# Query heads paired c with c+8 on the row halves of the array, and the decode value product on four column tiles

## The chip, the cores and the metric

The kernel runs on one core of one Trainium2 chip. A core has a matrix engine (TensorE, in the profile PE for its matmuls and PEld for its weight loads), a vector engine (DVE), an activation engine (ACT), GpSimd (POOL) and a queue engine that only issues transfers (SP). The metric is the time of one execution in microseconds (us), lower is better.

## What is computed

A two-layer decoder step for a prompt of 2048 tokens and for 64 sample tokens (8 sequences of 8). Layer 0 is a gated depthwise convolution of width 31. Then keys and values are made once, with 4 key heads of 64 numbers. Layer 1 has 16 query heads; query head h reads key head h // 4, over a window of 128 tokens, with one extra weight (a sink) per head in the softmax. The lines that matter here:

```python
# heads: N_HEADS = 16, N_KV_HEADS = 4, HEAD_DIM = 64, GROUP = 4, WINDOW = Q_BLOCK = 128
q = rms_norm(q.reshape(b, t, N_HEADS, HEAD_DIM), q_norm_g)
k = rms_norm(k.reshape(b, t, N_KV_HEADS, HEAD_DIM), k_norm_g)
s = jnp.einsum('bqkgd,bskd->bkgqs', qg, k_ctx) * (HEAD_DIM ** -0.5)
s = s - alibi_slopes()[..., None, None] * dist
s = jnp.where(allowed, s, -jnp.inf)
m = jnp.maximum(jnp.max(s, axis=-1, keepdims=True), sink)
p = jnp.exp(s - m)
p = p / (jnp.sum(p, axis=-1, keepdims=True) + jnp.exp(sink - m))
o = jnp.einsum('bkgqs,bskd->bqkgd', p, v_ctx)
return x + jnp.einsum('bte,ed->btd', o * jax.nn.silu(z), w_out)
```

## The kernel before

The program has three phases, one after another, and each engine runs an instruction list written out by hand; semaphores are the only thing that holds an engine back. Phase A is layer 0 up to the convolution. Phase B is the rest of layer 0, the keys and values and the queries; it writes queries (`q_d`), keys and values (`kv_d`) to memory, 17 tiles of 128 tokens (the last holds the 64 sample tokens). Phase C is the attention with the gate `z` and the output projection, 16 tiles of 128 prompt tokens. All large products are made of a high and a low part of both factors (`project`, 24 matmuls of 512 columns a call).

A tile `t` of phase C handles the 16 heads as four groups of four (`kv` 0 to 3). On TensorE the body of a tile runs: `qk` group 0 (scores), `z` first half (24 matmuls), `qk` group 1, `turn_p` group 0 (four transposes of the softmax), `z` second half, `pv` group 0 (value product, ahead of it two transposes of the gate), `qk` 2, `turn_p` 1, `out` of the tile before, first half, `pv` 1, `qk` 3, `turn_p` 2, `out` second half, `pv` 2, `turn_p` 3, then `turn_q` and `turn_k` for the next tile (8 and 4 transposes), `pv` 3. A score matmul needs its 64 key dimensions on the same half of the array's rows as its 64 query dimensions, and neighbouring query heads (2c and 2c+1) sit on the two halves. Both belong to one key head, so every key head is needed on both halves: `load_k` writes each key head twice (tile `c_kd`, two transfers a tile), `turn_k` transposes four 128x128 blocks of it into PSUM (`c_acc`), and ACT copies them into `c_kt` (`keys`). `c_kt` is a ring; on tiles with an even number the copy is made twice (slots 0 and 2). ACT does `queries(t+1)` and `keys(t+1)` one after the other, and `qk` of the next tile and its `z` wait for `kt_ready`.

Tiles 6 to 13 also carry one sample sequence each (b = 0 to 7): `decode_keys`, `decode_qk` (four products on tiles of 64 rows and 32 columns of the array), `decode_turn`, `decode_pv`, `decode_back`, with DVE and ACT steps in between. `decode_pv` multiplies the 128 rows of softmax (16 heads x 8 tokens) with all four value heads, 256 columns, although each row needs 64 of them; `decode_norm` then takes the four diagonal blocks out, one DVE instruction for each.

At the change from phase B to C the weights of the gate (`w_in_b`, 16 pieces of 128x512) are loaded, cut into high (ACT, `split_weights_hi`, line 101) and low parts (DVE, line 109), through four staging slots (`c`/`b_gate`) that SP fills when DVE has freed them. SP issues everything in order: between these pieces it also issues keys, `c_ht` and the store of the last queries.

Of the kernel before, what the change touches and what calls it, by code (L numbers as in the profile page):

```python
# [14 lines left out]
P = 128  # L15
# [64 lines left out]

def split_weights_dma(sp, weights, g, n0, k0=0, k1=KT):

    for k in range(k0, k1):
        piece = KT * n0 + k
        after(sp, g.w_lo, piece - g.stages + 1)
        sp.dma_start(g.stage[:, piece % g.stages], weights[k * P:(k + 1) * P, :]).then_inc(g.w_in[piece % g.stages], 16)

# [5 lines left out]

def split_weights_hi(act, m, gain, g, n0, free=None, k0=0, k1=KT):
# [9 lines left out]
def split_weights_lo(dve, m, gain, g, n0, k0=0, k1=KT):  # L104

    for k in range(k0, k1):
        piece = KT * n0 + k
        dve.wait_ge(g.w_hi, piece + 1)
        dve.scalar_tensor_tensor(g.wslot[m][:, 1, k], g.stage[:, piece % g.stages],  # L109
                                 gain_of(gain, k), f32(g.wslot[m][:, 0, k]),  # L110
                                 ALU.mult, ALU.subtract).then_inc(g.w_lo, 1)

# [658 lines left out]
def phase_b(nc, io, g, ctx, prev):  # L771
# [499 lines left out]
    def vector(dve, gates):  # L1271
# [90 lines left out]
        def queries(t):  # L1362
            n = rows_of(t)
            dve.wait_ge(qrs_ready, t + 1)
            rs = hrs[0:n, 0:HEADS].rearrange("p (h a) -> p h a", a=1).broadcast_to([n, HEADS, HD])
            given = qo if n == DEC else ps_q
            dve.tensor_tensor(heads(qo[0:n], HEADS), heads(given[0:n], HEADS), rs, ALU.mult).then_inc(q_ready, 1)

# [237 lines left out]
def phase_c(nc, io, g, ctx, prev):  # L1606
# [124 lines left out]
    def sync(sp):  # L1731
# [71 lines left out]
        def body(t, r):  # L1803
# [46 lines left out]
    def scalar(act):  # L1850
# [81 lines left out]
        def gates(first, stop):  # L1932
            w.stage = prev.gate_stage
            for k in range(first, stop):
                split_weights_hi(act, Z0 + k // KT, prev.gain, w, k // KT, k0=k % KT, k1=k % KT + 1)

# [68 lines left out]
    def vector(dve):  # L2005
# [13 lines left out]
        def scores(G, t, kv, b, r):  # L2019
# [3 lines left out]
            for j in range(GROUP):  # L2023
                if starts(t):
                    to, far, given = s[:, b, place(j)], dist[:, P:2 * P], ps_s[:, place(j), 0:P]
                else:
                    to = s[:, b:3:2 - b, place(j)]
                    far, given = (ap.rearrange("p (a n) -> p a n", a=2) for ap in (dist[:, :], ps_s[:, place(j)]))
                ins = dve.scalar_tensor_tensor(to, far, -slope[kv * GROUP + j], given, ALU.mult, ALU.add)  # L2029
            ins.then_inc(s_read, 1)  # L2030
# [86 lines left out]
        def decode_norm(b):  # L2117
            dve.wait_ge(d_pe, PE0 + PES * b + 4)
            dve.wait_ge(d_dve, DVE0 + DVES * b + 6)
            for kv in range(KVH):  # L2120
                rows = slice(kv * GROUP * DS, (kv + 1) * GROUP * DS)
                part = ps_tf[rows, CT * P + kv * HD:CT * P + (kv + 1) * HD].rearrange("p (a d) -> p a d", a=1).broadcast_to([GROUP * DS, 2, HD])
                ins = dve.tensor_scalar(sd[rows, 0:P].rearrange("p (a d) -> p a d", a=2), part, rdend[rows, 0:1], None, ALU.mult)
            ins.then_inc(d_dve, 1)

        def decode_gated(b):
# [3 lines left out]
            for e in range(2):  # L2130
                rows = slice(e * HD, (e + 1) * HD)
                part = szd[rows, :, b * DS:(b + 1) * DS]
                ins = dve.tensor_tensor(part, ps_t[rows, CT + 2].rearrange("p (k e i) -> p k e i", k=KT, e=2)[:, :, e], part, ALU.mult)
            ins.then_inc(d_dve, 1)
# [5 lines left out]
        def gates(first, stop):  # L2140
            w.stage = prev.gate_stage
            for k in range(first, stop):
                split_weights_lo(dve, Z0 + k // KT, prev.gain, w, k // KT, k0=k % KT, k1=k % KT + 1)

# [3 lines left out]
        ordered = lambda ap: ap.rearrange("p (g b a) -> p g b a", b=2, a=2)  # L2148
        given = sink0[:, :].rearrange("p (g a b) -> p g b a", b=2, a=2)
        dve.tensor_scalar(ordered(sink[:, :]), given, 1.0, None, ALU.mult).then_inc(nsink_made, 1)  # L2150
# [101 lines left out]
    def tensor(pe):  # L2252
# [7 lines left out]
        def turn_k(t, p):  # L2260
            pe.wait_ge(k_in[p], 32 * (t // 2 + 1) if isinstance(t, int) else t * 16 + (32 if p == 0 else 16))
# [57 lines left out]
        def qk(t, kv, r):  # L2319
# [4 lines left out]
            for a in range(2):  # L2324
                for half in range(2):
                    for e in range(2):
                        rows, h = slice(e * HD, (e + 1) * HD), kv * GROUP + 2 * a + e
                        keys = kt[rows, kv, window(t, r)].rearrange("p a n -> p (a n)")
                        to = ps_s[half * HD:(half + 1) * HD, place(2 * a + e), span_of(t, half)]
                        ins = pe.matmul(to, qt[rows, h // 2, half * HD:(half + 1) * HD], keys[:, span_of(t, half)], start=True, stop=True)  # L2330
            ins.then_inc(qk_done, 1)
# [9 lines left out]
        def pv(t, kv, r, loads):  # L2341
# [237 lines left out]
```

## Time and profile before

| | |
|---|---|
| median of three runs | 1718.73 us (1717.98, 1718.73, 1722.67) |
| the profiled execution's own time | 1717.28 us |
| its span, first to last instruction | 1715.5 us (1.8 us lie around it) |
| PE busy in the span | 1653.8 us (96%) |
| DVE, ACT, POOL busy | 1283.8, 778.2, 648.7 us |
| chain that ended last, by engine | PE 56%, POOL 24%, DVE 9%, issue 4%, DMA 3%, ACT 3% |
| of it line 121 on `c_acc` (z and out of phase C) | 16.0% |
| granted TensorE clock | 0.994 of full speed over the span |

Phase A lasts to about 590 us, phase B to about 1100, phase C from there. A busy share is read with care: matmuls overlap, so the question for a stage is not whether PE is busy but which wait ends last in it. That is what the chain of waits, the timeline of single engines and the starts of consecutive groups tell: the time from one group's start to the next group's start is what the first one costs its engine.

### The profile page before, as it was taken

To read this page: it belongs to the slowest core of one execution; us is meant where nothing else is said; L and a number is where in the kernel's file an instruction comes from. 1 tells how busy PE (TensorE), PEld (TensorE's weight loads), DVE (VectorE), ACT (ScalarE), POOL (GpSimd) and SP (SyncE) were. 2 spreads that over 40 slices of the span, in tenths; PEclk is the share of its full clock that TensorE was granted. 3 is DMA by queue.
4 is the path that set the end of the run, shared out by engine and by line. 5 is a ranking of instruction groups with operands and counts; after the bars stand their busy time and mean duration, and the time that the engine had idled before them with its cause. 6 is when DMAs were issued, how large, how long until landed. Compare 5 with 4: busy or idle time off the path is not lost.

```text
span 1715.5 us, 24728 instructions
## 1 busy us (share of the span) xinstructions
PE 1653.8 (96%) x9147; PEld 1352.0 (79%) x9147; DVE 1283.8 (75%) x1968; ACT 778.2 (45%) x1625; POOL 648.7 (38%) x504
## 2 busy tenths in 40 slices
PE   7999999999999988999999999888999999999998
PEld 6899888888898867888888888656777777777776
DVE  6479888998888657998898333567777777777774
ACT  6555556555644654343434342543333333333331
POOL 2489999999976304544454332100000000000000
PEclk9999999999999999999999999989999999999999
DMA  6411111121121655535554433744222333222321
GB/s 217 127 58 43 49 59 49 41 68 49 57 88 45 216 170 183 177 117 182 136 169 127 160 105 117 222 124 141 96 71 89 104 103 102 78 101 90 98 67 43
DMA packets 153714, 185.92 MB, mean 108 GB/s; under 512 B 51028, under 2 KB 116668, under 8 KB 149450
## 3 DMA queue, kind: packets, MB, share of 16 engines
q1 hardware_dynamic: 149274, 172.54, 31.7%
q10 hardware_dynamic: 4320, 11.80, 1.8%
q8 instruction: 73, 1.20, 0.3%
q14 instruction: 47, 0.39, 0.1%
HBM read 116.41 MB, written 70.72 MB: 109 GB/s over the span
## 4 chain that ended last, share of the span: by engine, by line
PE 56%; POOL 24%; DVE 9%; issue 4%; DMA 3%; ACT 3%; SPq 0%; POOLq 0%; DVEq 0%; ACTq 0%
POOL a_csum L489 22%; PE c_acc L121 16%; PE b_pso L121 13%; PE b_psq L121 9%; PE c_pso L2353 4%; PE a_ps L741 3%; PE c_pss L2330 2%; DVE a_pst L639 2%; POOL a_csum L486 2%; PE c_psp L2338 2%; DVE w L109 1%; DVE c_s L2029 1%; PE c_pso L2347 1%; PE c_pst L2257 1%; PE b_pst L1510 1%
## 5 line engine op out<-in xcount | busy, mean ns | idle before, releaser
L741 PE MATMUL a_ps<-a_xt,a_wring 128*128 128x512 f32 (+3 forms) x2880 | 556.9, 354 | 9.2 <-ACT a_zo L551 6.1
L741 PEld LDWEIGHTS a_ps<-a_xt,a_wring 128*128 128x128 f32 x2880 | 494.1, 189 | 65.5 <-ACT a_zo L551 7.7
L489 POOL TENSOR_TENSOR a_csum<-a_prod,a_csum 128x704 f32<-128x704 f32 (+1 forms) x231 | 404.9, 1753 | 43.1 <-ACT a_prod L538 10.0
L639 DVE SCALAR_TENSOR_TENSOR a_pst<-a_vbuf,taps,a_pst 128x704 f32<-128x704 f32 (+1 forms) x338 | 314.1, 929 | 10.4
L538 ACT ACTIVATE a_prod<-a_vbuf,taps 128x704 f32<-128x704 f32 (+1 forms) x252 | 214.7, 863 | 166.0 <-POOL a_csum L489 154.4
L121 PE MATMUL c_acc<-w,c_ht 128*128 128x512 f32 x768 | 183.4, 394 | 2.1 <-DVE c_sz L2017 0.7
L121 PE MATMUL b_pso<-w,b_yt 128*128 128x512 f32 x768 | 182.2, 393 | 1.2 <-DVE b_yt L1312 1.2
L121 PEld LDWEIGHTS c_acc<-w,c_ht 128*128 128x128 f32 x768 | 141.7, 188 | 38.4 <-issue 9.5
L121 PEld LDWEIGHTS b_pso<-w,b_yt 128*128 128x128 f32 x768 | 141.9, 188 | 30.1 <-DVE b_yt L1312 1.7
L1884 ACT ACTIVATE c_es<-c_es 128x4 f32<-128x4 f32 x64 | 13.2, 206 | 224.4 <-DVE c_es L2042 224.4
L1886 ACT ACTIVATE c_s<-c_s,c_nm 128x128 f32<-128x128 f32 x256 | 98.8, 387 | 0.1
L121 PE MATMUL b_psq<-b_w,b_ht 128*128 128x512 f32 x384 | 92.5, 395 | 5.5 <-DVE b_w L109 5.5
L121 PE MATMUL b_pso<-w,b_ht 128*128 128x512 f32 x384 | 91.5, 395 | 3.6 <-issue 3.6
L121 PE MATMUL b_psq<-w,b_ht 128*128 128x512 f32 x384 | 91.4, 393 | 0.0
L2029 DVE SCALAR_TENSOR_TENSOR c_s<-c_dist,c_pss 128x256 f32<-128x256 f32 (+1 forms) x256 | 88.2, 407 | 4.0 <-PE c_pss L2330 3.9
L121 PE MATMUL c_acc<-w,c_ot 128*128 128x512 f32 x360 | 86.0, 394 | 3.2 <-issue 3.2
L121 PEld LDWEIGHTS b_pso<-w,b_ht 128*128 128x128 f32 x384 | 73.0, 191 | 19.3 <-issue 3.8
L1400 DVE SCALAR_TENSOR_TENSOR b_conv<-b_three,taps,b_conv 128x704 f32<-128x704 f32 x90 | 86.6, 963 | 2.0
L121 PEld LDWEIGHTS b_psq<-b_w,b_ht 128*128 128x128 f32 x384 | 70.6, 188 | 21.8 <-DVE b_w L109 7.4
L121 PE MATMUL c_acc<-b_w,c_ot 128*128 128x512 f32 x360 | 86.4, 395 | 0.0
L121 PEld LDWEIGHTS b_psq<-w,b_ht 128*128 128x128 f32 x384 | 71.0, 188 | 15.6
L2052 DVE TENSOR_TENSOR c_pt<-c_psp,c_causal 128x512 f32<-128x512 f32 x124 | 79.9, 685 | 0.3
(247 smaller groups left out, 2257.0 us busy)
## 6 DMA issues: line engine op xcount, KB each, us to landing
ht_d<-b_ht SPq DMA_DIRECT2D x16, 1024.0 KB, 4.6
c_ht<-ht_d SPq DMA_DIRECT2D x16, 1024.0 KB, 5.0
a_stage<-in_w_in_a SPq DMA_DIRECT2D x24, 512.0 KB, 4.2
a_x<-in_x_prompt SPq DMA_DIRECT2D x16, 512.0 KB, 3.7
b_cz<-c_d SPq DMA_DIRECT2D x16, 512.0 KB, 5.4
b_cz<-z_d SPq DMA_DIRECT2D x16, 512.0 KB, 4.1
b_x<-in_x_prompt SPq DMA_DIRECT2D x16, 512.0 KB, 4.2
x_d<-b_x SPq DMA_DIRECT2D x16, 512.0 KB, 2.6
```

Of the source, the lines that this page charges most:

```text
L121: last = pe.matmul(out, xt[:, a, k, 0:n], w[:, b, k], start=(k == 0 and a == 0 and b == 0), stop=(k == KT - 1 and b == 1))
L486: pool.tensor_tensor(out, prod[:, PTAPS * n % RING, 0:t1 - t0], prod[:, (PTAPS * n + 1) % RING, 0:t1 - t0], ALU.add).then_inc(prod_added, 1)
L489: pool.tensor_tensor(out, prod[:, (PTAPS * n + i) % RING, 0:t1 - t0], out, ALU.add).then_inc(prod_added, 1)
L538: act.activation(prod[:, m % RING, 0:t1 - t0], vbuf[:, b % 2, t0 + k:t1 + k], ACT.Identity, scale=wcol(k, b), bias=bcol(b) if i == 0 else ...
L639: dve.scalar_tensor_tensor(part if k == DTAPS - 1 and not last else here, vbuf[:, b % 2, t0 + k:t1 + k], wcol(k, b), part if k == 0 else h ...
L741: last = pe.matmul(out, wring[:, u % 3, a, k], xt[c][:, e, k, 0:n], start=(k == 0 and a == 0 and e == 0), stop=(k == KT - 1 and a == 1))
L1400: dve.scalar_tensor_tensor(cw, win, w, cw, ALU.mult, ALU.add).then_inc(old_step, 1)
L1886: ins = act.activation(s[:, b, j], s[:, b, j], ACT.Exp, bias=nm[:, b, j:j + 1], accum_out=den[:, b, j:j + 1])
L2029: ins = dve.scalar_tensor_tensor(to, far, -slope[kv * GROUP + j], given, ALU.mult, ALU.add)
L2052: ins = dve.tensor_tensor(pt[:, half], ps_p[:, b], keep, ALU.mult)
L2330: ins = pe.matmul(to, qt[rows, h // 2, half * HD:(half + 1) * HD], keys[:, span_of(t, half)], start=True, stop=True)
L2353: ins = pe.matmul(ps_o[e * HD:(e + 1) * HD, 0:2 * P], v[:, half, kv * HD:(kv + 1) * HD], pt[:, half, 2 * e:2 * e + 2], start=(half == 0), ...
```

## The change

Head c is paired with head c+8 instead of 2c with 2c+1. Query heads c and c+8 read key heads c//4 and c//4+2, which lie 128 columns apart, so one 128x128 block of keys holds both in the order that the two row halves want. The keys are loaded once per head, `turn_k` makes two transposes, `c_kt` has two blocks in place of four, and ACT copies 256 columns where it copied 512. To match it, the query columns are written in pair order by DVE in phase B (one instruction as before, other strides), the rows of `w_out` are loaded in pair order (two blocks of 64 rows a piece), the gate's columns are loaded as two runs of 256 and written in pair order by two instructions a piece on ACT and two on DVE, and slopes, sinks and value heads are indexed to fit. Separately, `decode_pv` becomes eight matmuls of 32 output rows by 64 columns (four with 128 rows of cache, then four with the 8 new tokens), each on its own 32 columns of the array, all to the same 64 columns of PSUM, and `decode_norm` becomes one DVE instruction.

```diff
-def split_weights_dma(sp, weights, g, n0, k0=0, k1=KT):
+def split_weights_dma(sp, weights, g, n0, k0=0, k1=KT, part_of=None):
...
+def rows_of_pair(weights, k):
+    return weights.rearrange("(e k d) n -> k e d n", e=2, d=HD)[k]
+def columns_of_half(b):
+    return lambda weights, k: weights[k * P:(k + 1) * P, :].rearrange("r (e b n) -> b r e n", e=2, b=2)[b]
+def by_half(ap, e):
+    return ap[:, e * 2 * P:(e + 1) * 2 * P].rearrange("p (k d) -> p k d", d=HD)
+def by_pair(ap, e):
+    return ap.rearrange("p (k e d) -> p e k d", e=2, d=HD)[:, e]
...
-        act.activation(g.wslot[m][:, 0, k], g.stage[:, piece % g.stages], ACT.Copy, scale=gain_of(gain, k)).then_inc(g.w_hi, 1)
+        given, to = g.stage[:, piece % g.stages], g.wslot[m][:, 0, k]
+        if pairs:
+            act.activation(by_pair(to, 0), by_half(given, 0), ACT.Copy, scale=gain_of(gain, k))
+            given, to = by_half(given, 1), by_pair(to, 1)
+        act.activation(to, given, ACT.Copy, scale=gain_of(gain, k)).then_inc(g.w_hi, 1)
...
+        if pairs:
+            dve.scalar_tensor_tensor(by_pair(to, 0), by_half(given, 0), gain_of(gain, k), by_pair(high, 0), ALU.mult, ALU.subtract)
+            given, to, high = by_half(given, 1), by_pair(to, 1), by_pair(high, 1)
+        dve.scalar_tensor_tensor(to, given, gain_of(gain, k), high, ALU.mult, ALU.subtract).then_inc(g.w_lo, 1)
...
+            to = qo[:, :].rearrange("p (k e d) -> p e k d", e=2, d=HD)
+            dve.tensor_tensor(to, ps_q[:, :].rearrange("p (e k d) -> p e k d", e=2, d=HD), rs, ALU.mult).then_inc(q_ready, 1)
...
-    kt = at("c_kt", [P, KVH, 3, P], 12288 - 2 * g.slot_bytes)
+    kt = at("c_kt", [P, 2, 3, P], 12288 - 2 * g.slot_bytes)
-    kd = at("c_kd", [P, 2, KVH, 2, HD], prev.at["y"])
+    kd = at("c_kd", [P, 2, KV], prev.at["y"])
+    head = lambda kv, j: 2 * kv + j // 2 + HEADS // 2 * (j % 2)
...
-                sp.dma_start(kd[:, p, :, e], src.rearrange("n (h d) -> n h d", h=KVH)).then_inc(k_in[p], 16)
+                to = kd[:, p].rearrange("p (k e d) -> p e k d", k=2, e=2)[:, e]
+                sp.dma_start(to, src[:, e * P:(e + 1) * P].rearrange("n (k d) -> n k d", k=2)).then_inc(k_in[p], 16)
...
-            turned = acc[:, :].rearrange("p (h k) -> p h k", h=KVH)
+            turned = acc[:, 0:2 * P].rearrange("p (h k) -> p h k", h=2)
...
-            for kv in range(KVH):
-                rows = slice(kv * GROUP * DS, (kv + 1) * GROUP * DS)
-                part = ps_tf[rows, CT * P + kv * HD:CT * P + (kv + 1) * HD].rearrange("p (a d) -> p a d", a=1).broadcast_to([GROUP * DS, 2, HD])
-                ins = dve.tensor_scalar(sd[rows, 0:P].rearrange("p (a d) -> p a d", a=2), part, rdend[rows, 0:1], None, ALU.mult)
+            part = ps_tf[:, CT * P:CT * P + HD].rearrange("p (a d) -> p a d", a=1).broadcast_to([P, 2, HD])
+            ins = dve.tensor_scalar(sd[:, 0:P].rearrange("p (a d) -> p a d", a=2), part, rdend[:, 0:1], None, ALU.mult)
...
-            for h in range(KVH):
-                ins = pe.transpose(acc[:, h * P:(h + 1) * P], kd[:, p, h].rearrange("p e d -> p (e d)"), g.ident[:, :])
+            for k in range(2):
+                ins = pe.transpose(acc[:, k * P:(k + 1) * P], kd[:, p, k * P:(k + 1) * P], g.ident[:, :])
...
-            to = ps_tf[:, CT * P:CT * P + KV]
-            pe.matmul(to, ptd[:, 0], vd[:, b % 2], start=True, stop=False)
-            pe.matmul(to, ptd[0:DS, 1], vn[0:DS, b % 2], start=False, stop=True).then_inc(d_pe, 1)
+            for n, values in ((P, vd), (DS, vn)):
+                for kv in range(KVH):
+                    rows, dims = slice(kv * GROUP * DS, (kv + 1) * GROUP * DS), slice(kv * HD, (kv + 1) * HD)
+                    ins = pe.matmul(ps_tf[rows, CT * P:CT * P + HD], ptd[0:n, 0 if n == P else 1, rows],
+                                    values[0:n, b % 2, dims], start=(n == P), stop=(n == DS))
+            ins.then_inc(d_pe, 1)
...
-                        keys = kt[rows, kv, window(t, r)].rearrange("p a n -> p (a n)")
+                        keys = kt[rows, kv // 2, window(t, r)].rearrange("p a n -> p (a n)")
...
-                    ins = pe.matmul(ps_o[e * HD:(e + 1) * HD, 0:2 * P], v[:, half, kv * HD:(kv + 1) * HD],
+                    ins = pe.matmul(ps_o[e * HD:(e + 1) * HD, 0:2 * P], v[:, half, (kv // 2 + 2 * e) * HD:(kv // 2 + 2 * e + 1) * HD],
```

On TensorE, at the end of a tile (turns of the next tile's queries `c_q` and keys `c_kd`, then the last value product), before:

```order
L2338 MATMUL c_psp<-ident,c_s 128x128 x4
L2257 MATMUL c_pst<-ident,c_q 128x128 x8
L2263 MATMUL c_acc<-ident,c_kd 128x128 x4
L2347 MATMUL c_pso<-ident,c_sz 128x128 x2
L2353 MATMUL c_pso<-c_pt,c_v 64x256 x4
```

and after (line numbers move, the order does not):

```order
L2375 MATMUL c_psp<-ident,c_s 128x128 x4
L2291 MATMUL c_pst<-ident,c_q 128x128 x8
L2297 MATMUL c_acc<-ident,c_kd 128x128 x2
L2384 MATMUL c_pso<-ident,c_sz 128x128 x2
L2390 MATMUL c_pso<-c_pt,c_v 64x256 x4
```

Two transposes are gone between the query turns and the last value product. On TensorE, in a tile that carries a sample sequence, around its value product (`c_stg` holds the cached values, `c_vn` the new ones, `c_ptd` the turned softmax), before:

```order
L2330 MATMUL c_pss<-c_kt,c_qt 64x192 x8
L2338 MATMUL c_psp<-ident,c_s 128x128 x4
L2312 MATMUL c_pst<-c_stg,c_ptd 128x256
L2313 MATMUL c_pst<-c_vn,c_ptd 128x256
L121 MATMUL c_acc<-b_w_73,c_ot 128x512 x24
```

and after:

```order
L2367 MATMUL c_pss<-c_kt,c_qt 64x192 x8
L2375 MATMUL c_psp<-ident,c_s 128x128 x4
L2348 MATMUL c_pst<-c_stg,c_ptd 32x64 x4
L2348 MATMUL c_pst<-c_vn,c_ptd 32x64 x4
L151 MATMUL c_acc<-b_w_73,c_ot 128x512 x24
```

Two matmuls of 256 columns become eight of 64, in the same place. On ACT, at the change from phase B to C, where the gate's pieces (`b_gate`) are cut between the last queries (`b_squares`) and the first softmax (`c_es`, `c_s`), before:

```order
L1266 ACTIVATE b_pause<-b_qscale 128x1
L101 ACTIVATE w<-b_gate,cols 128x512 x2
L1884 ACTIVATE c_es<-c_es 128x4
L1886 ACTIVATE c_s,c_den<-c_s,c_nm 128x128 x4
L1878 ACTIVATE c_sz<-c_acc 128x512
L101 ACTIVATE w<-b_gate,cols 128x512 x2
L1186 ACTIVATE b_squares<-b_qo 64x1024
```

and after:

```order
L1296 ACTIVATE b_pause<-b_qscale 128x1
L127 ACTIVATE w<-b_gate,cols 128x4x64
L129 ACTIVATE w<-b_gate,cols 128x4x64
L127 ACTIVATE w<-b_gate,cols 128x4x64
L129 ACTIVATE w<-b_gate,cols 128x4x64
L1920 ACTIVATE c_es<-c_es 128x4
L1922 ACTIVATE c_s,c_den<-c_s,c_nm 128x128 x4
L1914 ACTIVATE c_sz<-c_acc 128x512
L127 ACTIVATE w<-b_gate,cols 128x4x64
```

Each piece is cut by two instructions of 256 columns where it was one of 512; nothing changes place.

## Rows read from the trace of the kernel before

**Rows 1.** Stage change: length, busy PE, PEld, DVE, ACT, POOL; PEclk, DMA share, GB/s

```profile
1090.00:1105.00 15.00, 12.62 (x73) 9.86 (x71) 10.31 (x22) 8.75 (x15) 1.82 (x3) 1.00 0.96 313
```

**Rows 2.** Chain of waits, end of tile 3 (start us, us, what)

```profile
1256.13 0.44 PE c_acc L2263 x4
...
1256.81 1.08 PE c_pso L2353 x8
1257.90 0.46 issue
```

**Rows 3.** Timeline of DVE there (start, us, operation [idle before <- releaser])

```profile
1255.14 0.42 DVE L2075 TENSOR_TENSOR c_sz<-c_pso,c_sz 128x256 f32<-128x256 f32 x1 [0.97 <-ACT c_sz L1892]
1255.48 1.28 DVE L2052 TENSOR_TENSOR c_pt<-c_psp,c_causal 128x512 f32<-128x512 f32 x2
```

**Rows 4.** Timeline of ACT there: the two copies of the keys

```profile
1257.18 0.59 ACT L1869 ACTIVATE c_kt<-c_acc 128x512 f32<-128x512 f32 x1
1257.66 0.60 ACT L1870 ACTIVATE c_kt<-c_acc 128x512 f32<-128x512 f32 x1
```

**Rows 5.** Waits in phase C (total us, times, longest)

```profile
PE c_pss L2330 <- issue: 1.4, 3, 0.5
```

**Rows 6.** Timeline of PE, start of tile 9 and of tile 10

```profile
1438.93 0.44 PE L2293 MATMUL c_pst<-ident,c_stg 128*128 128x128 f32 x2
1439.29 0.88 PE L2330 MATMUL c_pss<-c_kt,c_qt 64*64 64x192 f32 x16
...
1475.95 0.44 PE L2293 MATMUL c_pst<-ident,c_stg 128*128 128x128 f32 x2
1476.48 0.88 PE L2330 MATMUL c_pss<-c_kt,c_qt 64*64 64x192 f32 x16
```

**Rows 7.** Timeline of PE, tile 9: transposes, then the decode score product

```profile
1446.58 0.66 PE L2338 MATMUL c_psp<-ident,c_s 128*128 128x128 f32 x4
1447.17 0.44 PE L2300 MATMUL c_pst<-c_kdt,c_qdt 64*32 64x136 f32 x8
1447.53 5.74 PE L121 MATMUL c_acc<-w,c_ht 128*128 128x512 f32 x24
```

**Rows 8.** Timeline of PE, tile 9, later: value and score products, then decode value product

```profile
1453.71 0.44 PE L2347 MATMUL c_pso<-ident,c_sz 128*128 128x128 f32 x2 [0.23 <-DVE c_sz L2069]
1454.08 1.08 PE L2353 MATMUL c_pso<-c_pt,c_v 128*64 128x256 f32 x8
1455.10 0.88 PE L2330 MATMUL c_pss<-c_kt,c_qt 64*64 64x192 f32 x16
1455.91 0.66 PE L2338 MATMUL c_psp<-ident,c_s 128*128 128x128 f32 x4
1456.40 0.60 PE L2312 MATMUL c_pst<-c_stg,c_ptd 128*128 128x256 f32 x2
1456.93 0.69 PE L2313 MATMUL c_pst<-c_vn,c_ptd 8*128 8x256 f32 x2
1457.55 5.78 PE L121 MATMUL c_acc<-b_w,c_ot 128*128 128x512 f32 x24
```

**Rows 9.** Timeline of ACT at the stage change: two copies, then gate pieces

```profile
1078.49 0.38 ACT L1170 ACTIVATE b_three<-b_pso 128x256 f32<-128x256 f32 x1 [4.00 <-PE b_pso L121]
1078.77 0.38 ACT L1171 ACTIVATE b_three<-b_pso 128x256 f32<-128x256 f32 x1
1079.04 2.55 ACT L101 ACTIVATE w<-b_gate,cols 128x512 fp32r<-128x512 f32 x4
```

**Rows 10.** Chain of waits from the stage change to the end of tile 0

```profile
1094.73 8.88 DMA q_d<-b_qo
...
1106.24 1.23 ACT w L101 x2
...
1145.08 0.85 PE c_acc L2263 x4
...
1146.31 0.61 PE c_pso L2353 x4
```

More of the change, by code:

```diff
@@ L85, in split_weights_dma, with split_weights_hi @@
         after(sp, g.w_lo, piece - g.stages + 1)
-        sp.dma_start(g.stage[:, piece % g.stages], weights[k * P:(k + 1) * P, :]).then_inc(g.w_in[piece % g.stages], 16)
+        part = weights[k * P:(k + 1) * P, :] if part_of is None else part_of(weights, k)
+        sp.dma_start(g.stage[:, piece % g.stages], part).then_inc(g.w_in[piece % g.stages], 16)
+def rows_of_pair(weights, k):
[6 more added lines that the diff above has]
+    return ap.rearrange("p (k e d) -> p e k d", e=2, d=HD)[:, e]
 def gain_of(gain, k):
     return gain if isinstance(gain, float) else gain[:, k:k + 1]
-def split_weights_hi(act, m, gain, g, n0, free=None, k0=0, k1=KT):
+def split_weights_hi(act, m, gain, g, n0, free=None, k0=0, k1=KT, pairs=False):
     if free is not None:
@@ L100, in split_weights_hi, with split_weights_lo @@
         act.wait_ge(g.w_in[piece % g.stages], 16 * (piece // g.stages + 1))
[L101 to L104 removed]
+        given, to = g.stage[:, piece % g.stages], g.wslot[m][:, 0, k]
[3 more added lines that the diff above has]
+        act.activation(to, given, ACT.Copy, scale=gain_of(gain, k)).then_inc(g.w_hi, 1)
+def split_weights_lo(dve, m, gain, g, n0, k0=0, k1=KT, pairs=False):
     for k in range(k0, k1):
@@ L108, in split_weights_lo @@
         dve.wait_ge(g.w_hi, piece + 1)
-        dve.scalar_tensor_tensor(g.wslot[m][:, 1, k], g.stage[:, piece % g.stages],
-                                 gain_of(gain, k), f32(g.wslot[m][:, 0, k]),
-                                 ALU.mult, ALU.subtract).then_inc(g.w_lo, 1)
+        given, to, high = g.stage[:, piece % g.stages], g.wslot[m][:, 1, k], f32(g.wslot[m][:, 0, k])
+        if pairs:
+            dve.scalar_tensor_tensor(by_pair(to, 0), by_half(given, 0), gain_of(gain, k), by_pair(high, 0), ALU.mult, ALU.subtract)
+            given, to, high = by_half(given, 1), by_pair(to, 1), by_pair(high, 1)
+        dve.scalar_tensor_tensor(to, given, gain_of(gain, k), high, ALU.mult, ALU.subtract).then_inc(g.w_lo, 1)
 def project(pe, out, xt, w, n, lo_gate=None):
@@ L1365, in queries @@
             rs = hrs[0:n, 0:HEADS].rearrange("p (h a) -> p h a", a=1).broadcast_to([n, HEADS, HD])
-            given = qo if n == DEC else ps_q
-            dve.tensor_tensor(heads(qo[0:n], HEADS), heads(given[0:n], HEADS), rs, ALU.mult).then_inc(q_ready, 1)
+            if n == DEC:
+                dve.tensor_tensor(heads(qo[0:n], HEADS), heads(qo[0:n], HEADS), rs, ALU.mult).then_inc(q_ready, 1)
+                return
+            rs = hrs[:, 0:HEADS].rearrange("p (e k a) -> p e k a", e=2, a=1).broadcast_to([P, 2, HEADS // 2, HD])
+            to = qo[:, :].rearrange("p (k e d) -> p e k d", e=2, d=HD)
+            dve.tensor_tensor(to, ps_q[:, :].rearrange("p (e k d) -> p e k d", e=2, d=HD), rs, ALU.mult).then_inc(q_ready, 1)
         def convolve(j, h):
@@ L1934, in gates @@
             for k in range(first, stop):
-                split_weights_hi(act, Z0 + k // KT, prev.gain, w, k // KT, k0=k % KT, k1=k % KT + 1)
+                split_weights_hi(act, Z0 + k // KT, prev.gain, w, k // KT, k0=k % KT, k1=k % KT + 1, pairs=True)
         def turned():
@@ L2028, in scores @@
                     far, given = (ap.rearrange("p (a n) -> p a n", a=2) for ap in (dist[:, :], ps_s[:, place(j)]))
-                ins = dve.scalar_tensor_tensor(to, far, -slope[kv * GROUP + j], given, ALU.mult, ALU.add)
+                ins = dve.scalar_tensor_tensor(to, far, -slope[head(kv, j)], given, ALU.mult, ALU.add)
             ins.then_inc(s_read, 1)
@@ L2132, in decode_gated @@
                 part = szd[rows, :, b * DS:(b + 1) * DS]
-                ins = dve.tensor_tensor(part, ps_t[rows, CT + 2].rearrange("p (k e i) -> p k e i", k=KT, e=2)[:, :, e], part, ALU.mult)
+                ins = dve.tensor_tensor(part, ps_t[rows, CT + 2].rearrange("p (e k i) -> p e k i", k=KT, e=2)[:, e], part, ALU.mult)
             ins.then_inc(d_dve, 1)
@@ L2142, in gates @@
             for k in range(first, stop):
-                split_weights_lo(dve, Z0 + k // KT, prev.gain, w, k // KT, k0=k % KT, k1=k % KT + 1)
+                split_weights_lo(dve, Z0 + k // KT, prev.gain, w, k // KT, k0=k % KT, k1=k % KT + 1, pairs=True)
         prev.vector(dve, gates)
@@ L2326, in qk @@
                     for e in range(2):
-                        rows, h = slice(e * HD, (e + 1) * HD), kv * GROUP + 2 * a + e
-                        keys = kt[rows, kv, window(t, r)].rearrange("p a n -> p (a n)")
+                        rows = slice(e * HD, (e + 1) * HD)
+                        keys = kt[rows, kv // 2, window(t, r)].rearrange("p a n -> p (a n)")
                         to = ps_s[half * HD:(half + 1) * HD, place(2 * a + e), span_of(t, half)]
-                        ins = pe.matmul(to, qt[rows, h // 2, half * HD:(half + 1) * HD], keys[:, span_of(t, half)], start=True, stop=True)
+                        ins = pe.matmul(to, qt[rows, 2 * kv + a, half * HD:(half + 1) * HD], keys[:, span_of(t, half)], start=True, stop=True)
             ins.then_inc(qk_done, 1)
```

16 lines of the change are left out of this document (8 added, 8 removed).

## The prediction

> **What bounds the kernel now.** I read the page's busy shares first, then the chain of waits by line, then the timelines of single engines at the three places that the change touches. PE is busy for 96% of the span, and in phase C the chain runs along PE nearly without a break; a microsecond taken from PE there counts unless another engine holds the same spot. So each removed PE instruction has to be asked: what does the next one wait for? A tile with a sample sequence lasts 37.2 us (start of tile 9 to start of tile 10) [rows 6].
>
> At the end of each tile PE turns the next queries and keys, then runs the last value product. In [rows 2] the four key transposes take 0.44 us and the value product starts at 1256.81. [rows 3] show DVE at that moment: it writes the masked softmax that the product reads from 1255.48 to 1255.48 + 1.28 = 1256.76. The product starts 0.05 us after that. DVE in turn was started by ACT's copy of the product before (the idle 0.97 us in [rows 3]), and that chain contains no key transpose. PE and DVE arrive together; PE is not alone on the path here.
>
> After the value product PE stands for 0.46 us [rows 2], ahead of the next tile's scores. ACT ends the second copy of the keys at 1257.66 + 0.60 = 1258.26 [rows 4], and scores start at 1258.36 (the product's 1257.90 plus 0.46). So that wait belongs to the keys. There are three such waits in phase C [rows 5], at the tiles 2, 4 and 14, which have even numbers (two copies) and carry no sample sequence. In the even sample tiles two transposes of the cache stand in between and hide most of it: from them to the scores it is 0.53 us ahead of tile 10, against 0.36 ahead of tile 9, whose keys are copied once [rows 6]. The difference, 0.17, is still wait.
>
> In a sample tile PE waits once more, for DVE ahead of the first value product (0.23 us idle [rows 8]); that follows from the end of the first half of z through ACT and DVE and is not touched. From there on PE runs without idle time through the decode value product [rows 8].
>
> At the change from phase B to C the path is a chain of everything: transfers, ACT, DVE, the SP queue [rows 10]; the DMA engines are 96% busy for 15 us [rows 1].
>
> **The change part by part.**
>
> Key transposes: 2 of 4 go, 0.22 us of PE a tile. From tile 1 to tile 14 that would be 14 x 0.22 = 3.1 us. I take nothing: PE comes to the value product 0.22 us earlier and waits for DVE's 1256.76 instead [rows 2, 3]. The ends: 0 and 3.1, and the row stands next to 0. In tile 0 it is otherwise: there the four transposes take 0.85 us [rows 10], twice the 0.44 of [rows 2] (PE runs at the lower of its two clocks), and the value product, the gate copy and DVE follow one another on the chain. There 0.43 us are gained.
>
> Copies of the keys: 256 columns where it was 512. Two 256-column copies from PSUM on ACT start 0.28 us apart and take 0.38 [rows 9]; two of 512 start 0.48 apart and take 0.60 [rows 4]. The pair is done 0.28 + 0.38 = 0.66 us after its start, not 1.08: 0.42 earlier. Of the wait of 0.46 that leaves 0.04. Three tiles: 1.26. Four even sample tiles: 0.17 each, 0.68. Sum 1.9. The transposes end earlier too, but ACT gets to the keys only after the queries, so that adds nothing. From below: were a short copy as long as a long one, 0.
>
> Decode value product: two matmuls (four passes of 256 columns, each matmul being two passes) become eight (sixteen passes of 64 columns on four column tiles). The trace has a relative: the decode score product, four matmuls, eight passes of 136 columns on tiles of 32 columns. It and the four transposes ahead of it take 1447.53 - 1446.58 = 0.95 us, of which 0.59 are transposes and the change to small tiles, and 0.36 the product with the change back [rows 7]. Eight passes in 0.36 us: the four tiles work side by side, in two rounds. The value product with the same four transposes takes 1457.55 - 1455.91 = 1.64 [rows 8]. After the change it is 0.59 + two sets of four matmuls. At 136 columns a set is 0.36; at 64 it is less: four rounds of 256 columns take 1.02 us and four of 192 take 0.81 from start to start [rows 8], so 0.05 us a round for 64 columns. 72 columns fewer are 0.056 a round, 0.11 for two rounds, a set of 0.25. Between 0.25 and 0.36 I take 0.28, nearer the lower end, since both rounds stream fewer columns, and not on it, since the second round may wait for its weights. Then 0.59 + 0.56 = 1.15, a gain of 0.49 a sample tile (0.33 to 0.55), 8 x 0.49 = 3.9 us (2.6 to 4.4). What comes next, out of the tile before, waits for nothing; DVE's part afterwards shortens from four instructions to one, off the path.
>
> Gate pieces: one ACT instruction of 512 columns becomes two of 256, likewise on DVE. Four pieces take 2.55 us on ACT, some 0.61 each; two of 256 columns start 0.28 apart [rows 9], 0.56 a piece, which would be a gain of 0.05; with the full 0.38 for each it is 0.76, a loss of 0.15. The gate's pieces scale by a column of gains, which the 256-column rows do not, so I take the loss. On the chain lie two pieces from 1106.24 [rows 10] and two more after the first softmax: 4 x 0.15 = 0.6. Ahead of that the store of the last queries waits behind pieces in SP's queue; two or three such pieces lie ahead of it, up to 0.4 us, but the DMA engines are full [rows 1] and it lands only 8.88 us after its issue [rows 10], so I count 0.3. Together 0.9 (-0.2 to 1.5). SP's queue holds behind it the loads of the sample queries, the next `c_q` and keys; they move along. The gate's transfers have twice the descriptors, the keys' half the bytes; I count nothing, with 0.5 either way.
>
> Queries in pair order (DVE, as many elements), slopes, sinks, value heads, rows of `w_out`: same counts and sizes, nothing.
>
> Sum: -0.4 - 1.9 - 3.9 + 0.9 = -5.3 us. Against the profiled execution's 1717.28 that is 1712.0 (its span 1715.5 - 5.3 = 1710.2, with 1.8 around it). The median of the three runs is 1.45 us above that execution, which would give 1713.4; I say **1712.6**, in the middle. Its own range, with the ends of the terms, is -3.5 to -7.
>
> **The rivals.**
>
> B. The column tiles take turns: sixteen passes one after the other. For it speaks that no row has 128 rows by 32 columns. Against it: eight passes in 0.36 us [rows 7]. At 0.06 a pass (the 0.05 of 64 columns and a little) it is 0.59 + 0.96 + 0.1 = 1.65, as before; the gain of 3.9 is gone, -1.4 is left, 1716.5. The Trainium skill has a rule on this side ("TensorEngine Tiling (Array Packing)", Instruction Overhead): a matmul carries some 60 cycles of overhead, and "Don't take tiling factor from a dimension that's already small". By that rule 64 columns save next to nothing over the overhead; the score product's row does not show it at 136 columns, and no row shows 64.
>
> C. Slower: each of the sixteen passes waits for its own weights. A 128-column transpose, weights and all, costs 0.11 (0.44 for four [rows 2]); 16 x 0.11 = 1.76, with 0.59 ahead and some 0.15 for each of two more changes of tile shape that makes 2.65, 1.0 more than before, +8 us in eight tiles, 1724 after the other terms (+6.6). It decides from a product of about 2.5 us upwards. Against it the same row as in B.
>
> D. The transposes pay after all, since DVE is started earlier than I think: -3.1 more, 1709.
>
> E. It does not do what it says on ACT: copies of 256 columns from `c_acc` with a strided target are hardly shorter: -3.4, 1714.5; or the stage change costs 2 us more, about as much.
>
> **How the numbers follow.** Chances: forecast 0.64, B 0.18, D 0.09, C 0.05, E 0.04. The range runs from D (1709.5) to B with the median's offset (1717.5) and leaves out C and a forecast that is missed on the far side. 0.3% of the median, about what a measurement of this kernel can tell from no change, is 5.2 us; the forecast stands on that line. Of its 0.64 I put 0.43 beyond the line and 0.21 short of it. Faster: 0.43 + 0.09 = 0.52. Same: 0.21 + 0.18 + 0.04 = 0.43. Slower: 0.05.
>
> **What the profile after would show.** Right: in sample tiles the time from the four transposes to the start of out falls from 1.64 to 1.1 or 1.2; ahead of tiles 2, 4 and 14 the wait for the keys falls from 0.46 to under 0.1; the last value product of a tile starts as soon as DVE's masked softmax is done, with 0.2 to 0.3 us between PE's gate transposes and it that were not there before; tile 0 starts about a microsecond later. Wrong: a decode value product of 1.6 us or more (B, C); a last value product that starts 0.22 earlier against the product before it (D); key copies of 0.5 us or more (E); a longer stretch at half clock around the stage change, which I have not priced.

## The result, and the profile after

The changed kernel takes **1751.1 us** (median of four runs, 1749.0 to 1753.5) against 1719.2: a ratio of 1.0186 (95% interval 1.0170 to 1.0202), 32 us slower. 1712.6 was predicted, with 1709.5 to 1717.5 as the range. The profiled execution took 1750.37 us, its span is 1748.2. Of all executions reported below, a single one (1836.58 us, at a granted clock of 0.85) is left out of its kernel's median and ratio.

**Where the time is lost.** The gate's two pieces that stand at 1106.24 on the chain of [rows 10] start at 1106.87 now: 0.6 us late. DVE's masked softmax at the end of tile 3, at 1255.48 in [rows 3], starts at 1294.75 (below): 39.3 us late. Tile 9's scores, at 1439.29 in [rows 6], start at 1476.01: 36.7 late. The span ends 32.7 late. So 39 us are lost between 1107 and the end of tile 3, and the tiles behind win 6.6 back. PE's key transposes at the end of tile 0 start 16.8 us late (1144.87 and 1161.67), at the end of tile 1 39.8 late (1186.61 and 1226.37): the loss is in tiles 0 and 1.

The windows of that stretch, before and then after. Columns: length; busy time and instructions of PE, PEld, DVE, ACT, POOL; PEclk; DMA share; GB/s.

```profile
1130.00:1160.00 30.00, 26.65 (x160) 19.87 (x159) 18.11 (x40) 14.33 (x37) 0.00 (x0) 0.90 0.29 100
1160.00:1230.00 70.00, 64.51 (x426) 47.57 (x428) 51.26 (x122) 26.59 (x94) 0.00 (x0) 1.00 0.39 122
```

```profile
1130.00:1160.00 30.00, 19.65 (x104) 13.21 (x104) 13.37 (x37) 9.13 (x31) 0.00 (x0) 0.67 0.36 120
1160.00:1230.00 70.00, 49.19 (x270) 34.02 (x271) 34.33 (x78) 21.91 (x63) 0.00 (x0) 0.78 0.25 84
```

PE, DVE and ACT do less in the same time, and the DMA engines are a third full at most: no engine is the bound, all of them wait. The granted clock is 0.67 and 0.78 of full speed there; PE stands still again and again. What they wait for is in the chain of waits of the changed kernel (start, us, what; SPq is SP issuing a transfer):

```profile
1116.88 2.75 SPq L87
...
1119.67 4.80 SPq L1831
...
1125.17 8.68 DMA q_d<-b_qo
...
1140.68 5.56 SPq L87
1146.23 0.04 issue
1146.28 19.05 DMA c_stg<-in_w_out_b
...
1178.75 29.05 DMA c_stg<-in_w_out_b x2
```

The chain runs along the transfers of `w_out` (48 us in the two rows of `c_stg<-in_w_out_b`) and along SP's issues of them (line 87). ACT's timeline shows their pace; four of the sixteen pieces:

```profile
1181.00 0.63 ACT L129 ACTIVATE w<-c_stg 128x512 fp32r<-128x512 f32 x1 [3.60 <-DMA c_stg<-in_w_out_b]
1186.21 0.63 ACT L129 ACTIVATE w<-c_stg 128x512 fp32r<-128x512 f32 x1 [4.58 <-DMA c_stg<-in_w_out_b]
...
1202.61 0.63 ACT L129 ACTIVATE w<-c_stg 128x512 fp32r<-128x512 f32 x1 [4.10 <-DMA c_stg<-in_w_out_b]
1207.83 0.63 ACT L129 ACTIVATE w<-c_stg 128x512 fp32r<-128x512 f32 x1 [4.58 <-DMA c_stg<-in_w_out_b]
```

A piece comes every 5.2 us. The DMA view of that stretch gives the reason away: in tenths of the share of 16 engines, and in GB/s, for 40 slices of 1160 to 1200:

```profile
DMA  1111111111111111111111111111112111111113
GB/s 51 49 51 49 51 51 49 49 51 51 49 49 51 51 49 51 51 49 49 59 51 49 49 51 51 49 49 51 51 49 59 47 51 49 51 49 51 49 51 107
```

A piece of 128 x 512 numbers is 262,144 bytes; at 49 to 51 GB/s it takes 5.1 to 5.4 us. But for two slices at 59 and the last, which holds other loads, the queue is no faster than that, and it is never idle, at a share between one and two tenths of 16 engines. In [rows 1] 313 GB/s go with a share of 0.96, 20 GB/s an engine; by that 49 to 51 GB/s is what two or three engines carry. The packets in the trace say which: a row of 2 KB is one packet of 84 ns (median), and from 1162 to 1192 two packets are under way at once for 86% of the time, three for 13%. Two times 2048 bytes in 84 ns are 49 GB/s.

SP suffers in its turn. How long its instructions of this line and tensor take to issue (ns, minimum/median/maximum; first and last start), before, then after:

```profile
L86 SPq DMA_DIRECT2D c_stg<-in_w_out_b x16: 327/342/1537, 1108.1 to 1161.9; - x16
```

```profile
L87 SPq DMA_DIRECT2D c_stg<-in_w_out_b x16: 503/770/5557, 1109.0 to 1188.2; - x16
```

And SP's timeline, where what stands behind pieces is held up as well, before, then after:

```profile
1111.81 0.33 SPq L1791 DMA_DIRECT2D c_causal<-in_causal  x1
...
1117.68 0.49 SPq L918 DMA_DIRECT2D q_d<-b_qo  x1
```

```profile
1113.38 3.45 SPq L1827 DMA_DIRECT2D c_causal<-in_causal  x1
1116.88 2.75 SPq L87 DMA_DIRECT2D c_stg<-in_w_out_b  x1
1119.67 5.46 SPq L1831 DMA_DIRECT2D c_vn<-kv_d  x2
1125.17 0.60 SPq L948 DMA_DIRECT2D q_d<-b_qo  x1
```

The issue of `c_causal` went from 0.33 to 3.45 us. The store of the last queries (`q_d`), which tile 0 waits for on the chain above, goes out behind all this, 7.5 us later than before, and lands after 8.68 us in place of 2.9: some 13 of the 39 us. So semaphores are not the only thing that holds an engine back here: SP stands in its own issues.

**What the tiles gained.** The end of tile 3 after the change, on PE, DVE and ACT, against [rows 2 to 4]:

```profile
1295.24 0.38 PE L2297 MATMUL c_acc<-ident,c_kd 128*128 128x128 f32 x2
1295.46 0.38 PE L2384 MATMUL c_pso<-ident,c_sz 128*128 128x128 f32 x2
1296.08 1.08 PE L2390 MATMUL c_pso<-c_pt,c_v 128*64 128x256 f32 x8 [0.24 <-DVE c_pt L2088]
1297.20 0.88 PE L2367 MATMUL c_pss<-c_kt,c_qt 64*64 64x192 f32 x16
...
1294.75 1.28 DVE L2088 TENSOR_TENSOR c_pt<-c_psp,c_causal 128x512 f32<-128x512 f32 x2
...
1296.45 0.38 ACT L1905 ACTIVATE c_kt<-c_acc 128x256 f32<-128x256 f32 x1
1296.72 0.39 ACT L1906 ACTIVATE c_kt<-c_acc 128x256 f32<-128x256 f32 x1
```

PE is through its key transposes in 0.22 us (start to start) and stands 0.24 us for DVE, which was not there before. The key copies end at 1297.11, before the value product does, and the scores follow it after 0.04 us in place of 0.46. The decode value product in tile 9, against [rows 8]:

```profile
1492.61 0.66 PE L2375 MATMUL c_psp<-ident,c_s 128*128 128x128 f32 x4
1493.20 0.32 PE L2348 MATMUL c_pst<-c_stg,c_ptd 128*32 128x64 f32 x8
1493.45 0.31 PE L2348 MATMUL c_pst<-c_vn,c_ptd 8*32 8x64 f32 x8
1493.69 3.69 PE L151 MATMUL c_acc<-b_w,c_ot 128*128 128x512 f32 x15
```

From the four transposes to out 1.08 us in place of 1.64. From the key transposes at the end of tile 3 to those at the end of tile 14 PE takes 401.4 us before (1255.97 to 1657.41) and 395.1 after (1295.24 to 1690.31).

### The profile page after: what moved, and what is told of

Its sections match the earlier page's. It is cut to its first block, busy times and chain, and to the rows that moved or that the text cites. A ratio compares the mean times of both kernels' runs of the same rounds, so it can differ in the third digit from the quotient of the medians.

```text
span 1748.2 us, 24864 instructions
## 1 busy us (share of the span) xinstructions
PE 1658.9 (95%) x9211; PEld 1354.7 (77%) x9211; DVE 1279.2 (73%) x1960; ACT 778.0 (45%) x1641; POOL 648.9 (37%) x504
## 4 chain that ended last, share of the span: by engine, by line
PE 55%; POOL 23%; DVE 9%; DMA 6%; issue 3%; ACT 3%; SPq 2%; POOLq 0%; DVEq 0%; ACTq 0%
POOL a_csum L519 21%; PE c_acc L151 16%; PE b_pso L151 14%; PE b_psq L151 9%; PE c_pso L2390 4%; PE a_ps L771 3%; DMA c_stg<-in_w_out_b 3%; PE c_pss L2367 2%; DVE a_pst L669 2%; DVE c_pt L2088 2%; POOL a_csum L516 2%; PE c_psp L2375 1%; DMA q_d<-b_qo 1%; PE b_pst L1544 1%; PE a_pst L735 1%
## 5 line engine op out<-in xcount | busy, mean ns | idle before, releaser
L151 PEld LDWEIGHTS c_acc<-b_w,c_ot 128*128 128x128 f32 x360 | 67.7, 191 | 20.5 <-issue 5.9
```

What stands on the lines that cost most here:

```text
L151: last = pe.matmul(out, xt[:, a, k, 0:n], w[:, b, k], start=(k == 0 and a == 0 and b == 0), stop=(k == KT - 1 and b == 1))
```

## The experiments

Theory 1 is that the loss comes from how `w_out` is fetched: a transfer whose outer loop has two blocks (64 rows each, 512 rows apart) is carried by two DMA engines. Theory 2: it comes from the gate pieces in halves and the clock around the stage change. Theory 3: scattered rows are slow, whatever carries them. All ratios are to the kernel before, run on the same chip in the same set.

**The fetch alone, on the kernel before, in three doses.**

```diff
+def rows_of_blocks(weights, k):
+    return weights.rearrange("(e k d) n -> k e d n", e=2, d=P // 2)[k]
...
-        sp.dma_start(g.stage[:, piece % g.stages], weights[k * P:(k + 1) * P, :]).then_inc(g.w_in[piece % g.stages], 16)
+        part = weights[k * P:(k + 1) * P, :] if part_of is None else part_of(weights, k)
+        sp.dma_start(g.stage[:, piece % g.stages], part).then_inc(g.w_in[piece % g.stages], 16)
```

Only the pieces of `w_out` are fetched so; the other two have 4 and 16 where this has 2, in both places.

> The kernel before, with one edit: each piece of w_out (128 rows) is fetched by one transfer of two blocks of 64 rows, 512 rows apart, as in the changed kernel. The heads keep their old order, so the rows of w_out meet the wrong heads: that part of the computation is changed, its amount of work is not. Theory 1 (the two blocks confine the transfer to two DMA engines, 128 packets of 84 ns over 2 engines are 5.4 us a piece): +36 to +40 us on the kernel before, about 1757, with pieces copied every 5.2 us on ACT. Theory 2 (the loss comes from the gate pieces in halves and the lower clock around the stage change): 1717 to 1721. Theory 3 (rows fetched in scattered blocks are slow whatever engines carry them): about 1757, as theory 1.

> The kernel before, with each piece of w_out fetched by one transfer of four blocks of 32 rows, 256 rows apart (rows of w_out meet the wrong heads, as much work). Theory 1: four engines carry a piece, 128 x 84 / 4 = 2.7 us instead of 5.4; of the 16 pieces' extra time less than half stays and other work hides a part of that: 1722 to 1735. Theory 3: more blocks, no faster: 1757 or above. Theory 2: 1717 to 1721.

> The kernel before, with each piece of w_out fetched by one transfer of sixteen blocks of 8 rows, 64 rows apart (rows of w_out meet the wrong heads, as much work). Theory 1: sixteen engines carry it as in the kernel before: 1717 to 1721, no loss. Theory 3: scattered most of all, so 1757 or above. Theory 2: 1717 to 1721.

| blocks a piece | median, us | ratio (95% interval) |
|---|---|---|
| 1 (before) | 1718.12 | |
| 2 | 1756.88 | 1.0228 (1.0207 to 1.0248) |
| 4 | 1724.52 | 1.0040 (1.0026 to 1.0055) |
| 16 | 1719.93 | 1.0009 (0.9995 to 1.0023) |

The DMA view with four blocks, and with sixteen, 1160 to 1200:

```profile
DMA  0002222254322210045567899997000084019999
GB/s 10 0 0 49 86 104 98 106 113 142 115 105 100 96 28 0 0 97 173 127 172 176 356 414 298 390 401 303 0 0 0 0 360 164 0 42 253 340 393 315
```

```profile
DMA  6910398100005565799999500000750097999100
GB/s 188 303 33 0 66 334 192 20 8 0 0 2 126 170 148 136 238 369 372 343 326 418 246 16 0 0 0 16 291 225 8 0 209 209 389 357 254 25 0 0
```

Two blocks alone make the kernel before 39 us slower. Four blocks stream at 96 to 106 GB/s in the slices where little else is loaded, twice the 49 of two; four packets of 84 ns are then under way at once (for 81% of 1138 to 1142). Sixteen reach 188 and 303 GB/s in the first two slices, which hold rows of `w_out` alone (the peaks to the right are other loads), with most often sixteen packets under way, and cost nothing that can be told from noise, although their rows are the most scattered. Rate rises with the number of blocks: theory 1 holds, theory 3 falls. SP's longest issue of a piece goes the same way: 5.58 us with two blocks, 2.75 with four, 1.22 with sixteen, 1.54 in the kernel before.

**The changed kernel with its fetch mended.**

```diff
+        if part_of is rows_of_pair:
+            for e in range(2):
+                sp.dma_start(g.stage[e * HD:(e + 1) * HD, piece % g.stages], part_of(weights, k)[e]).then_inc(g.w_in[piece % g.stages], 16)
+            continue
...
```

ACT's wait counts, which change with it, are left out here.

> The changed kernel, with each piece of w_out fetched by two transfers of 64 rows in one block each; all the rest as changed. Theory 1: the loss is gone and what the tiles gained stays. From tile 2 to the end the trace of the changed kernel gains 6.5 us, tile 0 another 0.4, the stage change loses 1.1: 1719.2 - 5.8 = 1713.4 (1712 to 1715). Theory 2: 1749 to 1753, as the changed kernel. Theory 3: two blocks of 64 rows in two transfers are as scattered as in one: 1749 to 1753.

> The changed kernel with w_out's pieces in two transfers of 64 rows each, a second time, as the base that the other three runs of this set are set against: 1715 to 1718.

1716.25 us, ratio 0.9987 (0.9977 to 0.9998); the second time 1716.56, 0.9980 (0.9970 to 0.9990). The 35 us are gone: theory 2 falls. But 2.2 and 3.4 us of gain are less than the 5.8 that I expected. Not in the tiles behind: from the end of tile 3 to the end of tile 14 the first takes 395.1 us too. Its trace shows tile 1 later than I had counted. DVE and PE there before, then DVE, PE and the window behind them in this version:

```profile
1177.60 0.69 DVE L2082 TENSOR_TENSOR c_stg<-c_acc,c_stg 128x512 f32<-128x512 f32 x1 [3.85 <-DMA c_stg<-x_d]
...
1178.39 5.69 PE L121 MATMUL c_acc<-w,c_ot 128*128 128x512 f32 x24 [3.17 <-issue]
```

```profile
1181.56 0.69 DVE L2125 TENSOR_TENSOR c_stg<-c_acc,c_stg 128x512 f32<-128x512 f32 x1 [4.43 <-DMA c_stg<-x_d]
...
1182.35 7.29 PE L157 MATMUL c_acc<-w,c_ot 128*128 128x512 f32 x24 [3.75 <-issue]
...
1182.00:1186.00 4.00, 3.65 (x12) 2.92 (x13) 3.86 (x11) 0.14 (x2) 0.00 (x0) 0.72 0.65 262
```

DVE waits 4.43 us for the residual, which SP issues behind two cache loads; PE stands 3.75 us, its clock is then at 0.72 for 4 us, and 24 matmuls take 7.29 us where they took 5.69. Before, DVE's wait was 3.85 us, PE's 3.17, and the clock stayed at 1.0 in this execution.

**Fewer issues for SP.** Two pieces fetched together, 64 rows of both at a time, so that 16 issues do what 32 do in the version above.

```diff
+        for e in range(2):
+            sp.dma_start(g.stage[e * HD:(e + 1) * HD, slot:slot + 2], rows[e][:, k:k + 2]).then_inc(g.w_in[slot], 16)
...
```

A pair goes out when both its slots are free.

> The changed kernel, with two pieces of w_out fetched together: 64 rows of both at a time, so that SP issues 16 transfers for w_out as in the kernel before, where the base with two transfers a piece issues 32. If the extra 16 issues of some 0.5 us on SP cost time, 1 to 2.5 us below the base's 1716.4; if not, within 1 us of it.

1715.04 us, ratio 0.9977 (0.9964 to 0.9990), 4.0 us below before. Against the version with 32 issues that is 1.2 to 1.5 us less by the medians and 0.5 to 1.7 by the ratios, and the intervals overlap: a price of the issues is not shown. In the two profiled executions (spans 1712.5 and 1714.1) the clock accounts for the difference: here PE stands 2.31 us in tile 1, the clock holds, and the 24 matmuls take 5.72 us.

**The old decode value product** on the mended version.

```diff
+            to = ps_tf[:, CT * P:CT * P + KV]
+            pe.matmul(to, ptd[:, 0], vd[:, b % 2], start=True, stop=False)
+            pe.matmul(to, ptd[0:DS, 1], vn[0:DS, b % 2], start=False, stop=True).then_inc(d_pe, 1)
```

> The base (w_out in two transfers) with the decode value product and its normalization as in the kernel before: two matmuls of 256 columns, four rows of normalization. If the traces' difference of 0.57 us a sample tile is a gain of time: 8 x 0.57 = 4.5 us above the base, about 1721. Had the column tiles gained nothing (rival B of the prediction), 0 above it.

1721.74 us, ratio 1.0010 (1.0000 to 1.0020): 5.2 us above its base, with some 2.4 either way by the two intervals. In its trace tile 9 takes 1.64 us from the four transposes to out again (1463.03 to 1464.67). The new product is worth its 4.5 us, and rival B's zero falls.

**Four key transposes again.**

```diff
-            for k in range(2):
-                ins = pe.transpose(acc[:, k * P:(k + 1) * P], kd[:, p, k * P:(k + 1) * P], g.ident[:, :])
+            for k in (2, 3, 0, 1):
+                ins = pe.transpose(acc[:, k * P:(k + 1) * P], kd[:, p, k % 2 * P:(k % 2 + 1) * P], g.ident[:, :])
```

> The base, with four key transposes per tile again (the two that are needed, and the same two once more into columns that nobody reads). If DVE's masked softmax sets the start of a tile's last value product, two more transposes hide under it: 0.4 us above the base, from tile 0, at most 0.6. If PE set it (rival D), 14 x 0.22 + 0.4 = 3.5 us above the base.

1716.2 us (median of ten), ratio 0.9982 (0.9971 to 0.9993): 0.3 us above the base by the ratios, 0.4 below it by the medians, so no difference that can be told. PE at the end of tile 3, then DVE:

```profile
1264.30 0.60 PE L2304 MATMUL c_acc<-ident,c_kd 128*128 128x128 f32 x4
1264.74 0.38 PE L2391 MATMUL c_pso<-ident,c_sz 128*128 128x128 f32 x2
1265.15 1.08 PE L2397 MATMUL c_pso<-c_pt,c_v 128*64 128x256 f32 x8
...
1263.81 1.28 DVE L2095 TENSOR_TENSOR c_pt<-c_psp,c_causal 128x512 f32<-128x512 f32 x2
```

With four transposes the value product follows without a wait, with two it waits 0.24 us for DVE. In each of the three kernels it starts 1.33 to 1.34 us after DVE's masked softmax (1255.48 to 1256.81 before, 1294.75 to 1296.08 after, 1263.81 to 1265.15 here). The two that went were covered.

**The gate pieces alone**, on the kernel before: fetched in two parts, scaled by two instructions each, as in the diff of the change.

> The kernel before, with the gate pieces alone changed: fetched in two parts of 256 columns and scaled by two instructions of 256 columns on ACT and on DVE each (the gate's columns then meet the wrong heads; as much work). The prediction priced this at +0.9 us. The traces of the versions with w_out in two transfers stand 2 to 3 us later than those of the kernel before by tile 2, over and above what they ought to; if the halves are the cause, +2 to +3.5 us here. If it is the doubled number of transfers on SP, +1 at most here.

1720.35 us against 1719.36, ratio 1.0002 (0.9990 to 1.0014): 1.0 us by the medians, 0.3 by the ratio, and between 1.7 us of gain and 2.4 of loss. The forecast's 0.9 lies in it; the 2 to 3.5 us that I had come to suspect only at its edge. The version with PE reading the gate in pairs, and one instruction a piece again:

```diff
+def paired(ap):
+    return ap.rearrange("p (e k d) -> p k e d", e=2, d=HD)
...
-            last = pe.matmul(out, xt[:, a, k, 0:n], w[:, b, k], start=(k == 0 and a == 0 and b == 0),
+            last = pe.matmul(out, xt[:, a, k, 0:n], paired(w[:, b, k]) if pairs else w[:, b, k], start=(k == 0 and a == 0 and b == 0),
```

> The base, with the gate pieces scaled by one ACT and one DVE instruction of 512 columns as in the kernel before, and the order of pairs made where PE reads them: its moving operand has 512 columns in 8 x 2 runs of 64. The pieces' transfers keep their two parts. If halves cost 0.15 us a piece on ACT and as much on DVE, of which four pieces lie on the chain, 0.6 to 1.2 us below the base; if PE reads runs of 64 columns more slowly, above it by 24 matmuls x 16 tiles x 2 halves x the loss of one (10 ns would be 7.7 us).

1715.39 us, ratio 0.9968 (0.9955 to 0.9980); its base in the same set has 1716.56. It is 1.2 us faster by the medians, which the noise could make. PE loses nothing by reading runs of 64 columns: the 768 matmuls of the gate are busy for 184.6 us, 396 ns each, in its trace and in its base's.

**The residual first.** In tile 0 of SP's list:

```diff
                 sp.wait_ge(w.w_lo, 4 * KT)
+                load_res(0)
                 sp.wait_ge(d_pe, 3)
                 load_cache(0)
                 load_cache(1)
```

> The version with w_out in two transfers and PE reading the gate in pairs (1715.4), with one transfer moved: the first tile's residual is fetched ahead of the two cache loads instead of behind them. In the traces DVE stands 3.8 to 4.6 us for that transfer in tile 1, and PE's clock falls for some 4 us afterwards (1.6 us lost). Both gone: 4 to 6 us less, about 1710.5; if the next queries and keys, which then arrive behind the caches, take the wait over: 1 us less or none.

> The kernel before, with the same transfer moved. It waits 3.85 us for it; with that gone 3 to 5 us less, 1714 to 1716; if the next wait takes over, none. It tells how much of the gain of the version with the residual first has to do with the change at all.

On the mended version that reads the gate in pairs: **1709.67 us, ratio 0.9942 (0.9925 to 0.9960)**, 10 us below the kernel before and the fastest seen here. On the kernel before: 1715.84, ratio 0.9977 (0.9967 to 0.9988), 4 us. So of the ten, some four (2 to 6) have nothing to do with the pairing of heads. With the transfer moved in both, the mended change is worth 6.2 us, with some 3.5 either way by the two intervals. DVE and PE of the fastest version at that place:

```profile
1176.13 0.68 DVE L2131 TENSOR_TENSOR c_stg<-c_acc,c_stg 128x512 f32<-128x512 f32 x1
...
1177.44 4.82 PE L162 MATMUL c_acc<-w,c_ot 128*128 128x512 f32 x20
```

Neither waits any more; nor do they on the kernel before with the same move.

## Why the prediction was wrong, step by step

- **Rows of `w_out`: "same counts and sizes, nothing".** This step failed, and it alone accounts for the sign. Counts and sizes are the same indeed (128 packets of 2 KB), but the outer loop of the transfer went from 128 rows to 2 blocks, and with it the rate to 49 GB/s. Alone on the kernel before it costs 38.8 us; taken out of the changed kernel it gives 35 back. The prediction had no rival for it: it looked at what each transfer carries, not at how it is cut over engines. The Trainium skill would have told it. "DMA: Bandwidth & Descriptors", in "Why a DMA increments its semaphore by 16 and not by 1", says that a transfer uses the largest number of engines, up to 16, that divides the slowest dimension of size above 1 on both sides. By that rule 2 blocks get 2 engines and 4 get 4; the traces agree, with 49 to 51 and 96 to 106 GB/s, and with two and four packets under way at once.
- **Key transposes, 0 in tiles 1 to 14.** Right, and for the reason given: the wait of 0.24 us for DVE is there after, and two transposes more change the time by -0.4 to +0.3 us in all. Rival D would have given 3.5; it falls by the trace, and the two ratios leave open 2.9 at most (0.0002 with an interval of some 0.0015 either way). In tile 0, where 0.4 was forecast, PE goes from the key transposes to the value product in 0.99 us in place of 1.37 (1161.67 to 1162.66, and 1144.87 to 1146.24 before), with the granted clock at 0.54 and 0.59 there; no run prices this by itself.
- **Key copies, -1.9.** Right: copies of 256 columns take 0.38 and 0.39 us, and the wait of 0.46 is 0.04; rival E's 0.5 us a copy falls. In even sample tiles, transposes to scores: 0.37 ahead of tile 10 (1512.04 to 1512.41 on PE), against 0.53 in [rows 6]. This is read from the traces; no run puts the old copies back alone.
- **Decode value product, -3.9.** The direction was right, the size a little too small: 0.56 a sample tile and not 0.49, 4.5 us in eight. The two sets take 0.25 and 0.24 us, the low end of what was worked out. Rival B (0.06 us a pass) and C fall: eight passes in 0.25 us are 0.03 each. One can estimate what passes in turn would take: in [rows 8] two passes of 256 columns on the whole array take 0.53 us, so a pass of 64 some 0.07 at the same pace, and eight in turn 0.5. By that they overlap, two at a time at least; that it is four at a time, in two rounds, is not shown.
- **Stage change, +0.9.** Two 256-column instructions on ACT start 0.40 us apart (1106.87 and 1107.27), 0.80 a piece; the forecast had 0.76. Alone: +0.3 us, -1.7 to +2.4.
- **The sum.** The mended version with 16 issues stands at -4.0 (-6.2 to -1.7), an interval that holds the -5.3. The one with 32 issues stands at -2.2 (-4.0 to -0.3) and -3.4 (-5.2 to -1.7), short of it. The tiles behind tile 3 are not the reason: they gain 6.3 us in the traces of both versions. In tile 1 PE stands for the residual, a wait that was there before the change, and behind it the clock fell in the executions with 32 issues and not in the one with 16. With that wait gone on both sides the gain is 6.2, and the forecast's terms without the gate pieces, which that version does not halve, are -6.2; with 3.5 either way, so close a match is partly luck. What part of the rest is due to the issues and what to the clock is not settled.

## What to carry to other kernels

A change of layout is paid for where the data are fetched: of every transfer that a change re-cuts, compare the outermost dimension on both sides, not the bytes and packets only, and expect a transfer with 2 blocks to be slow: here 50 GB/s where 16 blocks reached 303. Two transfers of one block of 64 rows each, or one transfer of 16 blocks, cost nothing like it here. When a change loses more than any engine's work could explain, look for a constant GB/s in the DMA view: here a flat rate far below the peak was a queue on too few engines.

## What the runs showed of the hardware

- Rate by blocks, rows of 2 KB: 49 to 51 GB/s with two, 96 to 106 with four, up to 303 with sixteen; two, four and most often sixteen packets are under way at once.
- SP's issue is not free of what was issued before it: with the slow pieces outstanding single issues took up to 5.56 us, against 1.54 before, and the issue of a small load behind them 3.45 against 0.33; with four blocks a piece the longest took 2.75, with sixteen 1.22. What exactly the issue waits for, the trace doesn't say.
- PE that stood for 3.75 us had a granted clock of 0.72 over the next 4 us (a mean of its two levels, 1.2 and 2.4 GHz), and 24 matmuls took 7.29 us in place of 5.69. The length of this one wait does not tell whether the clock falls: among the traces it fell behind 2.44 us (sixteen blocks), 3.13 and more, and held behind 2.27, 2.31 and 3.17.
